# Modulation rows spread from memory, gates in ten buffers, both norms tile by tile, router with stationary weights

## The chip, the core and the metric

The kernel runs on one core of a Trainium2 chip. The metric is the time of one execution in device microseconds (us); lower is better. TensorE does the matrix products, VectorE and ScalarE the elementwise work and everything that leaves PSUM, GpSimd (POOL) small scalar work and part of the DMA issues, and SyncE (SP) issues the weight loads.

## The reference

One transformer layer over 640 tokens (128 of context, 512 latent), width 1024, in float32. The stages around the change are these:

```
mod   = silu(c) @ w_ada + b_ada            # six rows of 1024 for each of two conditions: sh1 sc1 g1 sh2 sc2 g2
z     = h @ w_in                           # queries, keys, values, and gate logits ga, gb
mix   = sigmoid(ga)*(oa @ w_proj_a) + sigmoid(gb)*(ob @ w_proj_b)
x1    = x + g1 * rms_norm(mix @ w_out, g_post_mix)
h2    = rms_norm(x1, g_pre_ffn) * (1 + sc2) + sh2
lg,le = h2 @ w_router_group, h2 @ w_router_expert      # 4 + 32 logits per token; top group, top 2 experts
y     = x1 + g2 * rms_norm(moe(h2), g_post_ffn)        # 32 SwiGLU experts of width 512
```

## The kernel before

The 640 tokens are five tiles of 128 rows (NT = 5); tile 0 is the context. Nothing is scheduled by a tool: each engine has its own hand-written program, and counting semaphores order them. TensorE executes strictly in program order, and so do the other engines. A product is done as three fp32r passes (hi x hi, lo x hi, hi x lo, L1120 to L1122). So each 1 MB piece of weights ("split" s) is first copied by ScalarE into a hi part (`split_hi`, L843) and then turned by VectorE into a lo part (`split_lo`, L1515). Four k-slices of one split against one tile are 12 matmuls with 512 moving columns.

The stages, with their place in the profiled execution:

1. Input projection and the modulation product, up to 325 us. The sigmoid gates leave PSUM through `zs` and are stored by POOL to memory (`gates_scratch`). The modulation columns are combined into `modr`, 128 x 64: four kinds of row, times two conditions, times 8 blocks.
2. Attention, 325 to 507.5 us: 40 steps (20 "diff", then 20 "swa"). The first exponential (L959) waits for the maximum (L1680) and for the landing of all stored gates; the maximum comes after a small exponential for lambda (L937).
3. TensorE spreads the modulation rows over the partitions: 12 groups of four matmuls (L1350) take one column of `modr`, broadcast to 128x128, against the identity, and ScalarE copies each bank to `brow` (L991).
4. Branch projections, splits 18 to 21, g = 0 to 3. VectorE multiplies each tile's bank by its gate (L1762, or L1765 and L1766 for the second branch). The gates come back from memory into `gst`, two buffers of 128x512, through POOL (L754): the load for tile m waits until VectorE has used tile m-2 (`mix_done`). Then ten groups of four transposes (L1377) turn the mix into columns, ScalarE makes hi (L1003), VectorE lo (L1773).
5. Out projection, splits 22 to 25, from 587.4 us. ScalarE copies each bank to `yrow` and squares it with a row sum (L1012, L1013).
6. The norms, each stage over all five tiles: VectorE adds the sums (L1779); POOL forms the inverse root by a scale and a power (L660, L661); VectorE scales by it and by the gate row g1 (L1783); POOL adds x (L764); ScalarE squares (L1020); POOL takes the second inverse root; VectorE scales and shifts (L1786, L1787); POOL stores h2 (L769).
7. Router: per tile eight transposes (L1401), two copies by ScalarE into the one buffer `h2T` (L1028), and eight float32 matmuls (L1406) that take the 128x128 block of h2 as stationary operand and move the 36 router columns. VectorE then selects experts (from L1792) and builds the gather tables.
8. Expert loop, from 735 to about 1324 us.
9. Last stage: the y pairs come back from memory, VectorE sums each pair (L1919, L1921). TensorE spreads the last gate rows g2 in four groups (L1498), and ScalarE copies them to `brow` (L1103). Behind these copies in ScalarE's program stand the squares (L1108). Then POOL's root, VectorE's scaling and addition of x (L1926, L1928), and the store.

## Time and profile before

| | us |
|---|---|
| median of 3 runs | 1379.41 |
| lowest and highest run | 1373.64, 1381.17 |
| the profiled execution's own time | 1375.16 |
| span of its trace | 1373.3 |
| TensorE busy | 1182.0 (86%) |
| VectorE busy | 866.5 (63%) |
| ScalarE busy | 695.7 (51%) |
| GpSimd busy | 324.1 (24%) |

The shares are averages over stages with different limits. The expert loop fills 43% of the span and is dense on TensorE and on the DMA engines; the stages 3 to 7, which the diff touches, take some 190 us before the first expert row table is built.

### The profile page before, as it was taken

To read this page: it belongs to the slowest core of one execution; us is meant where nothing else is said; L and a number is where in the kernel's file an instruction comes from. 1 tells how busy PE (TensorE), PEld (TensorE's weight loads), DVE (VectorE), ACT (ScalarE), POOL (GpSimd) and SP (SyncE) were. 2 spreads that over 40 slices of the span, in tenths; PEclk is the share of its full clock that TensorE was granted. 3 is DMA by queue.
4 is the path that set the end of the run, shared out by engine and by line. 5 is a ranking of instruction groups with operands and counts; after the bars stand their busy time and mean duration, and the time that the engine had idled before them with its cause. 6 is when DMAs were issued, how large, how long until landed. Compare 5 with 4: busy or idle time off the path is not lost.

```text
span 1373.3 us, 17096 instructions
## 1 busy us (share of the span) xinstructions
PE 1182.0 (86%) x6059; PEld 955.9 (70%) x6059; DVE 866.5 (63%) x941; ACT 695.7 (51%) x785; POOL 324.1 (24%) x300
## 2 busy tenths in 40 slices
PE   3889999998777989897545999999999999999941
PEld 2567787776565878785434888888888888888731
DVE  3443242124887633512554999999999999999836
ACT  3222233224544432132223777778778787787722
POOL 4022030000211001102402234444433333444200
PEclk9899999999997989998557999999999999999985
DMA  9533345551001003430134999999999999999924
GB/s 315 197 123 131 115 156 179 203 179 39 1 1 62 2 16 120 135 114 0 77 123 157 352 377 373 376 369 361 357 365 356 361 359 363 358 361 357 363 69 189
DMA packets 144845, 292.16 MB, mean 213 GB/s; under 512 B 11953, under 2 KB 13106, under 8 KB 144146
## 3 DMA queue, kind: packets, MB, share of 16 engines
q1 hardware_dynamic: 129936, 263.21, 53.9%
q0 software_dynamic: 14688, 28.12, 6.1%
q8 instruction: 37, 0.61, 0.2%
q14 instruction: 22, 0.18, 0.0%
q10 hardware_dynamic: 162, 0.05, 0.0%
HBM read 286.48 MB, written 27.92 MB: 229 GB/s over the span
## 4 chain that ended last, share of the span: by engine, by line
PE 67%; DVE 12%; ACT 7%; issue 7%; DMA 4%; POOL 1%; ACTq 0%; POOLq 0%; DVEq 0%
PE psum L1120 17%; PE psum L1122 16%; PE psum L1121 16%; DVE w_lo L1872 3%; DMA pt<-gates_scratch 2%; ACT w_hi L1038 2%; PE psum L1231 2%; PE psum L1334 2%; PE psum L1314 2%; PE psum L1138 2%; PE psum L1406 1%; ACT L1055 1%; ACT act_hi L1049 1%; PE psum L1432 1%; PE psum L1462 1%
## 5 line engine op out<-in xcount | busy, mean ns | idle before, releaser
L1120 PE MATMUL psum<-w_hi,act_hi 128*128 128x512 f32 (+1 forms) x1288 | 515.2, 400 | 21.4 <-DVE w_lo L1872 6.4
L1122 PE MATMUL psum<-w_hi,act_lo 128*128 128x512 f32 (+1 forms) x1288 | 501.6, 389 | 0.0
L1121 PE MATMUL psum<-w_lo,act_hi 128*128 128x512 f32 (+1 forms) x1288 | 500.8, 389 | 0.0
L1120 PEld LDWEIGHTS psum<-w_hi,act_hi 128*128 128x128 f32 x1288 | 244.0, 189 | 94.0 <-issue 18.1
L1122 PEld LDWEIGHTS psum<-w_hi,act_lo 128*128 128x128 f32 x1288 | 243.7, 189 | 51.2
L1121 PEld LDWEIGHTS psum<-w_lo,act_hi 128*128 128x128 f32 x1288 | 244.5, 190 | 44.7
L1872 DVE TENSOR_TENSOR w_lo<-raw_extra,w_hi 128x2048 fp32r<-128x2048 f32 x96 | 217.3, 2290 | 45.8 <-ACT w_hi L1038 45.8
L1872 DVE TENSOR_TENSOR w_lo<-raw_mix,w_hi 128x2048 fp32r<-128x2048 f32 x96 | 218.9, 2289 | 12.2 <-ACT w_hi L1038 12.1
L1038 ACT ACTIVATE w_hi<-raw_mix 128x2048 fp32r<-128x2048 f32 x96 | 183.8, 1916 | 26.7 <-PE psum L1122 26.7
L1038 ACT ACTIVATE w_hi<-raw_extra 128x2048 fp32r<-128x2048 f32 x96 | 180.7, 1913 | 6.2 <-PE psum L1122 6.2
L1515 DVE TENSOR_TENSOR w_lo<-raw_mix,w_hi 128x2048 fp32r<-128x2048 f32 (+1 forms) x26 | 57.4, 2208 | 176.1 <-ACT w_hi L843 176.1
L797 POOL DMA_INDIRECT y_scratch<-ysb,scatter_column x32 | 34.5, 1078 | 357.3 <-DVE ysb L1896 324.0
L785 POOL DMA_INDIRECT xg<-h_scratch,gather_column x32 | 71.0, 2219 | 25.5 <-POOL gather_column L782 25.5
L843 ACT ACTIVATE w_hi<-raw_mix 128x2048 fp32r<-128x2048 f32 (+1 forms) x26 | 48.0, 1846 | 49.7 <-DMA raw_mix<-in_w_in 26.6
L1314 PE MATMUL psum<-ident,rows 128*128 128x128 f32 x204 | 39.7, 303 | 25.3 <-DVE rows L529 10.2
L959 ACT ACTIVATE rows<-psum,soft 128x640 f32<-128x640 f32 (+3 forms) x80 | 50.6, 641 | 12.2 <-DVE soft L1682 7.4
L792 POOL COPY scatter_column<-scatter_rows 128x1 uint32 (+1 forms) x32 | 54.6, 1706 | 0.2
L782 POOL COPY gather_column<-gather_rows 128x1 uint32 (+1 forms) x32 | 53.1, 1658 | 5.0 <-PE psum L1432 4.9
L1049 ACT ACTIVATE act_hi<-psum 128x1024 fp32r<-128x1024 f32 x32 | 32.8, 1026 | 37.8 <-PE psum L1432 37.8
L973 ACT ACTIVATE pt<-psum 128x512 f32<-128x512 f32 (+2 forms) x36 | 18.5, 514 | 61.8 <-PE psum L1314 61.4
L1314 PEld LDWEIGHTS psum<-ident,rows 128*128 128x128 f32 x204 | 25.0, 155 | 33.4 <-issue 16.2
L1680 DVE TENSOR_REDUCE soft<-psum 128x2 f32<-128x1280 f32 (+3 forms) x40 | 44.4, 1110 | 4.6 <-PE psum L1290 2.5
(264 smaller groups left out, 1263.5 us busy)
## 6 DMA issues: line engine op xcount, KB each, us to landing
raw_mix<-in_w_e SPq DMA_DIRECT2D x96, 1024.0 KB, 8.3
raw_extra<-in_w_e SPq DMA_DIRECT2D x96, 1024.0 KB, 8.3
raw_mix<-in_w_in SPq DMA_DIRECT2D x16, 1024.0 KB, 5.9
raw_mix<-in_w_ada SPq DMA_DIRECT2D x16, 1024.0 KB, 7.3
ada_first<-in_w_ada SPq DMA_DIRECT2D x8, 1024.0 KB, 20.1
gates_scratch<-rows POOLq DMA_DIRECT2D x20, 256.0 KB, 3.3
pt<-gates_scratch POOLq DMA_DIRECT2D x20, 256.0 KB, 3.6
raw_mix<-in_w_out SPq DMA_DIRECT2D x4, 1024.0 KB, 5.1
```

What stands on the lines that cost most here:

```text
L782: po.tensor_copy(idx_g[:, par:par + 1], tab_g[:, bass.ds(n, 1)]).then_inc(gi_done, 1)
L785: po.indirect_dma_start(out=xg[:, par * D:(par + 1) * D], out_offset=None, in_=h2_d, in_offset=bass.IndirectOffsetOnAxis(idx_g[:, par:par ...
L792: po.tensor_copy(idx_s[:, par:par + 1], tab_s[:, bass.ds(n, 1)]).then_inc(si_done, 1)
L843: ac.activation(whi(s % HL)[:, :, 0:w], raw(n % RAW_MIX)[:, :, 0:w], ACT.Copy).then_inc(hi_done, 1)
L959: ac.activation(e[:, m * w:(m + 1) * w], s_view(i)[:, m, :], ACT.Exp, bias=soft[:, 16 * b + m:16 * b + m + 1], scale=SCALE, accum_out=tota ...
L1038: ac.activation(whi(hl), raw(slot), ACT.Copy).then_inc(hi_done, 1)
L1120: pe.matmul(out, a_hi(ka_), w_hi[:, kw, :], start=s, stop=False)
L1121: pe.matmul(out, a_hi(ka_), w_lo[:, kw, :], start=False, stop=False)
L1122: ins = pe.matmul(out, a_lo(ka_), w_hi[:, kw, :], start=False, stop=e)
L1314: ins = pe.transpose(bank(6)[:, x * P:(x + 1) * P], src[:, kt * P:(kt + 1) * P], ident[:, :])
L1515: ve.tensor_tensor(wlo(s % HL)[:, :, 0:w], raw(n % RAW_MIX)[:, :, 0:w], whi(s % HL)[:, :, 0:w].bitcast(F32), ALU.subtract).then_inc(lo_don ...
L1872: ve.tensor_tensor(wlo(hl), raw(slot), whi(hl).bitcast(F32), ALU.subtract).then_inc(lo_done, 1)
```

## The change

- **Modulation rows.** `modr` (columns 0 to 63) is transposed once, by TensorE between the second and the third score step of attention, copied by ScalarE to `arow` ahead of the lambda exponential, and stored by POOL to `modulation_rows_scratch` (8 x 1024). After attention POOL issues six loads that read one row of 4 KB for each of 128 partitions (512 KB each), ahead of gate load number 10. Two more such loads fetch the g2 rows after the out projection. The matmuls of L1350 and L1498 and the copies of L991 and L1103 are gone.
- **Gates.** `gst` lies in `yrow`, ten buffers. Loads 0 to 9 wait for the last diff scores; load m from 10 on waits for the use of tile m-10.
- **Mix transposes** of tile i-1 follow the product of tile i in the last group, with ScalarE's hi and VectorE's lo parts of the same tile.
- **Norms.** Each tile goes by itself: `new_x(i)` and `new_h(i)` on VectorE, the addition of x included; POOL adds the two sums and takes both roots of one column; ScalarE's square of x1 tile i-1 stands behind the copies of tile i of the last split.
- **Router.** Two `h2T` buffers and four banks for the transposes; the weights are the stationary operand (36 columns), h2 moves 128 columns; the 36x128 result is copied and transposed back. TensorE's order is written out.

The core of the diff:

```diff
-        gst = pt[:, 0:1024].rearrange("p (b n) -> p b n", b=2)
+        gst = yrow[:, :].rearrange("p (b n) -> p b n", b=GATE_SLOTS)          # GATE_SLOTS = 10
+        h2T_v = [h2T[:, :], pt[:, 0:D]]
...
 @block.gpsimd
+            po.wait_ge(b_cp, 1)
+            po.dma_start(mod_d.rearrange("r (k p) -> (r k) p", p=P), arow[0:64, 0:P]).then_inc(mod_out, 16)
...
+            for m in range(4 * NT):
+                g, i = m // NT, m % NT
+                branch, n, slot = g % 2, g // 2, m % GATE_SLOTS
+                if m == 0:
+                    po.wait_ge(s_done, NDIFF)
+                if g == 0:
+                    po.wait_ge(gate_out[i], 64)
+                if m == GATE_SLOTS:
+                    po.wait_ge(pv_done, NSTEP)
+                    po.wait_ge(mod_out, 16)
+                    for r in range(6):
+                        po.dma_start(br_v[:, r, :], mod_d[r].partition_broadcast(P)).then_inc(b_in, 16)
+                if m >= GATE_SLOTS:
+                    po.wait_ge(mix_done, m - GATE_SLOTS + 1)
+                po.dma_start(gst[:, slot, :], gates_d[...]).then_inc(g_in[slot], 16)
...
+            for i in range(NT):
+                po.wait_ge(y_cp, 5 + i + 1)
+                link(po.tensor_tensor(stat[:, i:i + 1], stat[:, 48 + i:49 + i], stat[:, 53 + i:54 + i], ALU.add))
+                rsqrt(stat[:, 8 + i:9 + i], stat[:, i:i + 1], 1, 1.0 / D).then_inc(yrs, 1)
+                po.wait_ge(x1sq, i + 1)
+                rsqrt(stat[:, 40 + i:41 + i], stat[:, 32 + i:33 + i], 1, 1.0 / D).then_inc(x1rs, 1)
+                if i:
+                    store_h2(i - 1)
+            store_h2(NT - 1)
+            po.wait_ge(tile_mm, 5 * NS)
+            for r in range(2):
+                po.dma_start(g2_v[:, r, :], mod_d[6 + r].partition_broadcast(P)).then_inc(g2_in, 16)
...
 @block.scalar
+            ac.wait_ge(b_tr, 1)
+            ac.activation(arow[0:64, 0:P], bank(7)[0:64, 0:P], ACT.Copy).then_inc(b_cp, 1)
             ac.wait_ge(lam_sum, 1)
             ac.activation(lamv[:, 2:4], lamv[:, 0:2], ACT.Exp).then_inc(lam_exp, 1)
...
+            for i in range(NT):
+                merged_rows(1, i)
+                if i:
+                    x1_squares(i - 1)
+            h2_columns(0)
+            h2_columns(1)
+            x1_squares(NT - 1)
+            h2_columns(2)
+            logit_rows(0)
+            h2_columns(3)
+            for i in range(1, NT - 1):
+                logit_rows(i)
+            h2_columns(NT - 1)
+            logit_rows(NT - 1)
...
 @block.tensor
             scores(1)
+            pe.wait_ge(mod_done, 1)
+            pe.transpose(bank(7)[0:64, 0:P], modr[:, :], ident[:, :]).then_inc(b_tr, 1)
             scores(2)
...
-            for m in range(12):                      # and four matmuls each: modr column, identity
...
+                    if g == 3 and i:
+                        transpose_mix(i - 1)
+            transpose_mix(NT - 1)
...
+            def router(i):
...
+                    ins = pe.matmul(bank(2 + i % 2)[0:NR, 0:P], wr_v[:, k, :], h2T_v[i % 2][:, k * P:(k + 1) * P], ...)
+            def logits(i):
+                pe.wait_ge(rt_cp, i + 1)
+                pe.transpose(bank(7)[:, i * NR:(i + 1) * NR], rlT[...], ident[0:NR, 0:NR]).then_inc(rl_done, 1)
+            transpose_h2(0); transpose_h2(1); router(0); transpose_h2(2); router(1); logits(0)
+            transpose_h2(3); router(2); logits(1); router(3); logits(2); logits(3)
+            transpose_h2(4); router(4); logits(4)
...
 @block.vector
+            def new_x(i):
+                ve.wait_ge(yrs, i + 1)
+                link(ve.scalar_tensor_tensor(yr[:, i, :], yr[:, i, :], stat[:, 8 + i:9 + i], br_v[:, min(i, 1), :], ...))
+                ve.wait_ge(x2_in[i], 16)
+                ve.tensor_tensor(xrow[:, i, :], xrow[:, i, :], yr[:, i, :], ALU.add).then_inc(x1_done, 1)
+            def new_h(i):
+                ve.wait_ge(x1rs, i + 1)
+                link(ve.scalar_tensor_tensor(yr[:, i, :], xrow[:, i, :], stat[:, 40 + i:41 + i], br_v[:, 2 + min(i, 1), :], ...))
+                ve.tensor_tensor(yr[:, i, :], yr[:, i, :], br_v[:, 4 + min(i, 1), :], ALU.add).then_inc(h2_done, 1)
+            ve.wait_ge(b_in, 16 * 6)
+            for i in range(NT):
+                new_x(i)
+                if i:
+                    new_h(i - 1)
+            new_h(NT - 1)
+            ve.wait_ge(h2t_done, 2 * NT)
+            ve.wait_ge(rt_mm, NT - 2)
+            ve.tensor_copy(h2T_v[(NT - 1) % 2][:, 512:1024], bank(h2_bank(NT - 1, 1))).then_inc(h2t_v, 1)
```

## Rows read from the trace of the kernel before

**Rows 1.** The page: the span, and the granted TensorE clock in 40 slices.
```profile
span 1373.3 us, 17096 instructions
...
PEclk9899999999997989998557999999999999999985
```

**Rows 2.** Chain that ended last, whole span: start us, length us, what.
```profile
326.16 2.62 DMA gates_scratch<-rows
...
507.58 13.19 PE psum L1350 x96
...
691.89 1.77 PE psum L1401 x8
694.33 3.64 PE psum L1406 x16
...
1343.91 5.80 PE psum L1498 x32
```

**Rows 3.** Waits from 505 to 740: total us, times, longest.
```profile
DVE rows L1762 <- DMA pt<-gates_scratch: 17.7, 6, 5.3
...
DVE osq L1765 <- DMA pt<-gates_scratch: 10.3, 6, 3.2
```

**Rows 4.** Busy time and granted clock by stretch, seven columns of the windows view.
```profile
508.00:510.00 2.00, 2.00 (x11) 2.00 (x11) 0.69 (x1) 0.43 (x2) 0.00 (x0) 0.50 0.32 119
...
512.00:514.00 2.00, 2.00 (x20) 2.00 (x19) 0.00 (x0) 1.18 (x2) 0.00 (x0) 1.00 0.00 0
...
690.00:698.00 8.00, 7.28 (x33) 6.73 (x33) 0.00 (x1) 1.19 (x2) 0.00 (x0) 0.50 0.30 82
```

**Rows 5.** ScalarE in order of time, from 505 to 740.
```profile
631.24 0.60 ACT L1012 ACTIVATE yrow<-psum 128x512 f32<-128x512 f32 x1 [13.19 <-PE psum L1122]
...
642.12 0.60 ACT L1012 ACTIVATE yrow<-psum 128x512 f32<-128x512 f32 x1 [1.40 <-PE psum L1122]
```

**Rows 6.** VectorE in order of time, from 505 to 740.
```profile
675.95 1.22 DVE L1787 TENSOR_TENSOR yrow<-yrow,brow 128x1024 f32<-128x1024 f32 x1
698.00 0.35 DVE L1792 TENSOR_TENSOR router_logits<-psum,br 128x180 f32<-128x180 f32 x1 [20.82 <-PE psum L1406]
```

**Rows 7.** One line's instructions: duration ns minimum, median, maximum.
```profile
L1783 DVE SCALAR_TENSOR_TENSOR yrow<-yrow,stat,brow x5: 1280/3356/3364, 645.2 to 654.2; 128x1024 f32<-128x1024 f32 x5
...
L764 POOL TENSOR_TENSOR rows<-rows,yrow x5: 2340/3313/3319, 646.6 to 659.7; 128x1024 f32<-128x1024 f32 x5
```

**Rows 8.** Groups of GpSimd instructions: busy us, mean ns of one.
```profile
L661 POOL TENSOR_TENSOR stat<-stat,half 128x5 f32<-128x5 f32 x4 | 4.8, 1194 | 0.3
...
L769 POOL DMA_DIRECT2D h_scratch<-yrow x5 | 2.8, 555 | 10.5 <-DVE yrow L1787 10.5
...
L660 POOL TENSOR_SCALAR stat<-stat 128x5 f32<-128x5 f32 x4 | 0.8, 196 | 93.6 <-DVE stat L1779 55.3 <-ACT pt L1108 29.1 <-ACT squares_scratch_a L863 8.0
```

**Rows 9.** DMA issues: KB each, median us to landing.
```profile
pt<-gates_scratch POOLq DMA_DIRECT2D x20, 256.0 KB, 3.6
...
rows<-in_x_sample POOLq DMA_DIRECT2D x4, 512.0 KB, 4.4
...
lam<-in_lam_q POOLq DMA_DIRECT2D x2, 32.0 KB, 5.7
```

**Rows 10.** ScalarE, then VectorE, from 322 to 350.
```profile
325.89 1.28 ACT L937 ACT_TABLE_LOAD   x1
...
329.26 0.37 ACT L959 ACTIVATE rows<-psum,soft 128x128 f32<-128x128 f32 x1 [1.88 <-DVE soft L1682]
...
327.42 0.16 DVE L1672 TENSOR_TENSOR lamv<-lamv 128x1 f32<-128x1 f32 x1 [11.16 <-ACT lamv L937]
```

**Rows 11.** ScalarE, then VectorE, from 1308 to the end.
```profile
1355.18 1.06 ACT L1108 ACTIVATE pt<-raw_extra 128x1024 f32<-128x1024 f32 x1
1356.14 0.19 ACT L1108 ACTIVATION_READ_ACCUMULATOR pt<-raw_extra 128x1 f32 x1
...
1352.22 1.28 DVE L1921 SCALAR_TENSOR_TENSOR raw_extra<-raw_extra,pair_weights 128x1024 f32<-128x1024 f32 x1
```

More of the change, by code:

```diff
@@ L986, in _ @@
                 attention_hi(ac, q)
[L989 to L999 removed]
+            for x in range(20, 24):
+                split_hi(x)
             for m in range(2 * NT):
@@ L1096, in _ @@
                     a_round(r)
-            for m in range(4):
-                ac.wait_ge(g2_mm, m + 1)
-                if m == 0:
-                    ac.wait_ge(all_scattered, 1)
-                ac.activation(br_v[:, m // 2, (m % 2) * 512:(m % 2) * 512 + 512], bank(m), ACT.Copy).then_inc(g2_cp, 1)
             for i in range(NT):
@@ L1340, in _, with transpose_mix @@
                 out_transpose(pe, q_)
-            pe.wait_ge(mod_done, 2)
             wait_emptied(pe, len(uses) - 1)
-            for m in range(12):
-                if m >= 2:
-                    pe.wait_ge(b_cp, m - 1)
-                for x in range(4):
-                    col = (m // 2) * 8 + (m % 2) * 4 + x
-                    ins = pe.matmul(bank(5 + m % 2)[:, x * P:(x + 1) * P], modr[:, col:col + 1].broadcast_to([P, P]), ident[:, :], start=True, stop=True)
-                ins.then_inc(b_tr, 1)
+            def transpose_mix(i):
+                pe.wait_ge(mix_done, 15 + i + 1)
+                for m in range(2 * i, 2 * i + 2):
+                    if m < 3:
+                        pe.wait_ge(o_cp, NOUT)
+                    else:
+                        pe.wait_ge(mh_done, m - 2)
+                        pe.wait_ge(ml_done, m - 2)
+                    for x in range(4):
+                        k = 4 * (m % 2) + x
+                        ins = pe.transpose(bank(5 + m % 3)[:, x * P:(x + 1) * P], xrow[:, i, k * P:(k + 1) * P], ident[:, :])
+                    ins.then_inc(mt_done, 1)
             for g in range(4):
@@ new lines, in router @@
+            def router(i):
+                pe.wait_ge(h2t_cp, min(2 * i + 2, 2 * NT - 1))
+                if i == NT - 1:
+                    pe.wait_ge(h2t_v, 1)
+                if i >= 2:
+                    pe.wait_ge(rt_cp, i - 1)
+                for k in range(KD):
+                    ins = pe.matmul(bank(2 + i % 2)[0:NR, 0:P], wr_v[:, k, :], h2T_v[i % 2][:, k * P:(k + 1) * P], start=(k == 0), stop=(k == KD - 1))
+                ins.then_inc(rt_mm, 1)
+            def logits(i):
+                pe.wait_ge(rt_cp, i + 1)
+                pe.transpose(bank(7)[:, i * NR:(i + 1) * NR], rlT[:, i % 2 * P:(i % 2 + 1) * P], ident[0:NR, 0:NR]).then_inc(rl_done, 1)
@@ L1409, in _ @@
+            transpose_h2(0)
+            transpose_h2(1)
+            router(0)
+            transpose_h2(2)
+            router(1)
+            logits(0)
+            transpose_h2(3)
+            router(2)
+            logits(1)
+            router(3)
+            logits(2)
+            logits(3)
+            transpose_h2(4)
+            router(4)
+            logits(4)
             pe.wait_ge(m_ready, 1)
@@ L1492, in _ @@
                     a_round(r)
-            pe.wait_ge(all_scattered, 1)
-            for m in range(4):
-                for x in range(4):
-                    col = 48 + (m // 2) * 8 + (m % 2) * 4 + x
-                    ins = pe.matmul(bank(m)[:, x * P:(x + 1) * P], modr[:, col:col + 1].broadcast_to([P, P]), ident[:, :], start=True, stop=True)
-                ins.then_inc(g2_mm, 1)
         @block.vector
@@ L1749, in _, with mix_low @@
                 attention_lo(ve, q)
+            def mix_low(i):
+                for m in range(2 * i, 2 * i + 2):
+                    j = m % 2
+                    ve.wait_ge(mh_done, m + 1)
+                    d = (slice(None), slice(4 * j, 4 * j + 4), slice(i * P, (i + 1) * P))
+                    ve.tensor_tensor(al[d], bank(5 + m % 3).rearrange("p (k n) -> p k n", k=4), ah[d].bitcast(F32), ALU.subtract).then_inc(ml_done, 1)
             split_lo(20)
```

182 lines of the change are left out of this document (70 added, 112 removed).

## Prediction

> **What bounds the kernel now.** I read the page first: a span of 1373.3 us, and a TensorE clock that falls in three places, early in attention, around 640 to 740 us and at the end [rows 1]. The diff leaves the expert loop alone, so the question is what it takes out of the stretch from 505 to 740 us and out of the tail. Therefore the chain that ended last comes next [rows 2]. The 48 matmuls that spread the modulation rows stand on it with 13.19 us, each tile of the router with 1.77 us of transposes and 3.64 us of products, and the last spreading with 5.80 us. The waits say what stops the branch projections: VectorE waits 17.7 + 10.3 = 28.0 us in all for gates to land [rows 3], because with two buffers each load of 3.6 us [rows 9] is issued only when the gate two tiles back has been used. The norms are a chain by nature; here all five tiles pass each stage before the next begins. From the last product (642.12, when ScalarE can take its bank [rows 5]) to the router logits on VectorE (698.00 [rows 6]) TensorE does nothing but the router, and 55.9 us pass. That is the largest piece to win.
>
> **Attention's start (loss of 0.6).** TensorE's one transpose and ScalarE's copy now stand ahead of ScalarE's table load of 1.28 us and the lambda exponential. They need the second score step, so VectorE gets lambda about 1.4 us later than its 327.42 [rows 10]. But the first exponential, at 329.26 [rows 10], was released by the last gate store, which left at 326.16 and took 2.62 us [rows 2], to 328.8. VectorE's maximum was ready some 0.8 us before the exponential. So about 0.6 of the 1.4 us comes through; between 0 and 3 us, the upper end if the longer pause makes the clock dip last longer. All later steps shift by it. The store of 64 rows on POOL and the first ten gate loads, about 0.55 us of POOL each, run under attention, where POOL has nothing else but one head norm per tile.
>
> **From attention to the out projection (gain 17.4).** The 13.19 us [rows 2] go. The products then start at 507.6 in the same low clock: 0.50 from 508 to 510, 1.00 from 512 [rows 4]. What ran slowly there was the spreading; now it is products, and about 3.9 us at half rate cost them 2.0 us. A tile of a split takes (642.12 - 631.24) / 4 = 2.72 us at full clock [rows 5], so 20 tiles of branch projection take 54.4 us. The 20 tiles of the out projection took as long before 642.1, so that stage began at 587.7, and the stretch before it, from 507.6, took 80.1 us. In its place stand 54.4 + 2.0, then 40 transposes, at half of the 0.22 us that one takes at the low clock (1.77 / 8 [rows 2]), 4.4, and about 1.9 us of stalls: the first mix tile must wait for split 23's lo part, and the last tile's transposes wait for its own mix, two VectorE operations of some 0.7 us (half of the 1.22 for 1024 columns [rows 6]) and one ScalarE copy of 0.60 [rows 5]. Sum 62.7, gain 17.4. Interleaved transposes could stall up to 1 us a tile more, or nothing; I keep 14 to 19.
>
> This needs gate 10 by about 540 and the modulation rows by about 617. POOL issues six broadcast loads at 505, then the gates as their buffers come free. A plain load of 512 KB lands after 4.4 us, while a small one that repeats a row (32 KB in 256-byte pieces) takes 5.7 us [rows 9]. No row shows a broadcast with 4 KB pieces. Like plain loads, six are over 10 to 27 us after their issue, by 532. By bytes at the rate of the 32 KB load, one would take 91 us. I take the plain load: the piece is 4 KB in both, while the 5.7 us of the small load are nearly the same as the 4.4 us of one sixteen times its size and so tell of a fixed cost. Hidden then, with 8 us or more to spare.
>
> **Out projection and norms.** The projection is untouched and ends at 642.1 - 17.4 + 0.6 = 625.3; the last split's tile 0 is ready at 614.4. ScalarE needs about 1.3 us for copy and square (0.60 each, and a readout). POOL's first root is now an addition and a scale of 0.2 each and a power of 1.19 [rows 8], 1.8 us with its links. For one column I assume what five columns cost, since 0.2 us for five values is all fixed cost. So VectorE's `new_x(0)` starts at 617.5 and takes 1.28 + 1.22 = 2.5 [rows 6, 7]. The addition of x, 2.3 to 3.3 us on POOL [rows 7], has become 1.22 on VectorE.
>
> Then each tile is a circle, because POOL's program puts the second root of tile i before the first root of tile i+1: new_x 2.5, square 1.3 (1.06 and 0.19 [rows 11]), root 1.55, store of h2 0.65 (0.555 [rows 8] and its link), first root of the next 1.8: 7.8 us. Meanwhile VectorE runs `new_h` of the tile before, 2.5 us. Do they disturb each other? Rows 7 show it: VectorE's scaling takes 1.28 us alone and 3.36 beside POOL's addition, and POOL's addition 2.34 alone and 3.31 beside VectorE. Each is longer by what was left of the other. So POOL's root, which would begin 1.3 us after new_x, begins when new_h is over, 2.5 us after it: 9.0 us a circle.
>
> The Trainium skill (SBUF — State Buffer, "SBUF: two separate sides") says the same: a VectorE operation with two SBUF inputs and a GpSimd operation that reads SBUF shut each other out for a whole instruction. This rule speaks against the new order; without it the circle is 7.8.
>
> With 9.0: new_x(1) at 624.7 (no new_h or store yet), the next at 633.7, 642.7 and 651.7; new_h(3) to 656.7, the last root to 658.3, new_h(4) to 660.8. Before, the last h2 tile was ready at 675.95 + 1.22 = 677.2 [rows 6]. So of the 16.8 us won earlier 16.4 are left here: the norms are no shorter in themselves, but the router can start inside them.
>
> **Router.** ScalarE's copies of h2 tiles 0 and 1 stand behind the square of x1 tile 3 (to 646.5), so the first product starts at 647.8. A product moves 128 columns in eight matmuls. From the spreading, 48 matmuls of that shape in 13.19 us, 3.9 of them at half rate [rows 2, 4], one is 0.23 us at full and 0.46 at low clock: 1.8 or 3.6 us a tile. At the low clock that is nothing won over the 3.64 [rows 2]. All at low clock: products 0 and 1 to 656.8, tile 3's transposes (1.8 us) behind new_h(3), products 2 and 3 to 666.8, tile 4's transposes to 669.3, a copy, product 4 to 673.6, copy and transpose back: 674.4. At full clock from the second product on, the two late tiles bound it: 666.6. Which? The old router, with 36 moving columns, was busy 7.28 of 8 us and stayed at 0.50 [rows 4]; the spreading, 128 columns without a break, rose to 1.00 after about 4 us [rows 4]. Here tiles 0 to 2 are 9 us without a break, but then comes a pause of 2 to 3 us. I take the middle, 670.5: gain at this point 698.0 - 670.5 = 27.5.
>
> The skill's page TensorE: Matmul & The Clock Gate (Part 1) lets the clock follow how busy TensorE is. By that the old router too should have run at 1.00, and rows 4 contradict it; by the page the new one ends at 666.6, and the sum would be 4 us better.
>
> **Expert tables, loop and tail.** The tables and the gathers follow VectorE's logits unchanged. SP's loads into the overlapped buffers now wait for all router logits instead of the transposed copies, still some 26 us before the tables are ready. The loop is the same. In the tail VectorE's last pair sum ends at 1352.22 + 1.28 = 1353.5 [rows 11]; the last square then ends at 1354.8 instead of 1356.37: gain 1.6. The 5.80 us of spreading were mostly under the loads of y, so more isn't to be had.
>
> **Sum.** 27.5 + 1.6 = 29.1. On the profiled execution's 1375.2 (span 1373.3 and 1.9 around it) this gives 1346.1; the median of the runs, 1379.4, is 4.2 higher, and with it 1350.3. I predict 1350.
>
> **Rivals.**
> - *No shutting out.* POOL's small operations slip in beside new_h: circle 7.8, the router starts 2.3 us earlier and at full clock ends at 663. Gain 32 to 36, time 1343 to 1347. For it: these operations are short. Against: rows 7. Chance 0.22.
> - *A leaner win.* The attention dip costs 3, stalls in the last branch group 3, the low clock holds through the router: gain 14 to 22, time 1357 to 1365. Chance 0.15.
> - *Broadcast loads are slow* (the side slower than before). Gate 10 and its followers stand behind six loads on one queue. If each takes t, gate 10 lands at 505 + 6t + 4; it is needed at 540, so loss begins at t = 5 us if they don't overlap, and eats the whole 29 us at t = 10 us. Slower by over 0.5% from t = 11. At the 91 us of the upper bound the time would be near 1860. For it: nothing but that no row has such a load. Chance 0.06; a further 0.05 that it, or the circle of five engines' waits, leaves the gain between -7 and 7.
> - The forecast, 1346 to 1356: chance 0.52.
>
> About 0.5%, 7 us, is what a measurement can tell from no change. Faster 0.89, same 0.06, slower 0.05. The range of 1340 to 1363 takes in the first two rivals and the bounds of the clock and leaves out the slow loads.
>
> **What the new profile would show.** Products start within 1 us of attention's last copy; no VectorE wait for gates; the out projection starts near 571; new_x starts 8 to 9 us apart, with POOL's scale right behind new_h; the first router product near 648; VectorE's logits near 670 (667 if the clock row shows 1.00, 674 if 0.50); the expert loop as long as before. I am wrong if gates after number 9 are waited for, if new_x starts are 11 us apart, or if the loop's length changes.

## The result and the profile after

The changed kernel takes 1335.5 us in the median of four runs (1331.97 to 1336.06), the kernel before 1379.3 beside it: ratio 0.968 with a 95% interval of 0.965 to 0.972. The profiled execution took 1335.54 us, 39.6 less than that of before, and its span is 39.7 shorter. I had predicted 1350 with a range of 1340 to 1363, so the time is lower than the range.

To see where the 39.7 us lie, both spans are cut at the same instructions: ScalarE's last copy of a gate bank (325.27 before), VectorE's last copy of attention (506.74), ScalarE's copy of the last split's tile 0 (631.24 in [rows 5]), VectorE's logits (698.00 in [rows 6]), and the end. The cuts that no row above shows, kernel before (ScalarE, then VectorE) and changed kernel:

```profile
325.27 0.60 ACT L929 ACTIVATE rows<-psum 128x512 f32<-128x512 f32 x1 [2.12 <-PE psum L1122]
506.74 0.69 DVE L531 COPY rows<-psum 128x512 f32<-128x512 f32 x1 [1.21 <-PE psum L516]
```
```profile
322.78 0.60 ACT L950 ACTIVATE rows<-psum 128x512 f32<-128x512 f32 x1 [2.12 <-PE psum L1152]
...
508.18 0.69 DVE L538 COPY rows<-psum 128x512 f32<-128x512 f32 x1 [1.21 <-PE psum L523]
...
615.03 0.60 ACT L1024 ACTIVATE yrow<-psum 128x512 f32<-128x512 f32 x1 [13.19 <-PE psum L1152]
```

| stretch | before | after | difference | predicted |
|---|---|---|---|---|
| start to last gate copy | 325.27 | 322.78 | -2.5 | 0 |
| to attention's last copy | 181.47 | 185.40 | +3.9 | +0.6 |
| to the last split's tile 0 | 124.50 | 106.85 | -17.65 | -17.4 |
| to the router logits | 66.76 | 45.82 | -20.9 | -10.7 |
| to the end | 675.30 | 672.75 | -2.55 | -1.6 |
| sum | 1373.3 | 1333.6 | -39.7 | -29.1 |

The page of the changed kernel: the span and the granted TensorE clock in 40 slices. Against [rows 1] the dip around 640 to 700 is one slice shorter, and the middle of attention is a little lower.

```profile
span 1333.6 us, 16867 instructions
...
PEclk9899999999887898999858999999999999999985
```

VectorE in order of time, changed kernel, from 612 to 665. It answers [rows 6] and the first line of [rows 7]:

```profile
617.67 1.28 DVE L1833 SCALAR_TENSOR_TENSOR yrow<-yrow,stat,brow 128x1024 f32<-128x1024 f32 x1 [13.50 <-POOL stat L669]
...
630.84 1.28 DVE L1833 SCALAR_TENSOR_TENSOR yrow<-yrow,stat,brow 128x1024 f32<-128x1024 f32 x1 [2.45 <-POOL stat L669]
...
634.62 1.23 DVE L1840 TENSOR_TENSOR yrow<-yrow,brow 128x1024 f32<-128x1024 f32 x1
...
638.30 1.28 DVE L1833 SCALAR_TENSOR_TENSOR yrow<-yrow,stat,brow 128x1024 f32<-128x1024 f32 x1 [2.46 <-POOL stat L669]
...
660.85 0.34 DVE L1855 TENSOR_TENSOR router_logits<-psum,br 128x180 f32<-128x180 f32 x1 [2.66 <-PE psum L1446]
```

`new_x` (L1833) comes every 638.30 - 630.84 = 7.46 us, not every 9.0. Each time VectorE has waited some 2.45 us for GpSimd's root. (The first two, with no `new_h` or store between them, are 5.73 us apart, where I had 7.2.) What GpSimd does in one such circle (L781 adds the sums, L668 is the scale, L669 the power, L777 the store), changed kernel, GpSimd in order of time:

```profile
634.66 1.23 POOL L668 TENSOR_SCALAR stat<-stat 128x1 f32<-128x1 f32 x1 [3.85 <-ACT pt L1031]
635.97 0.54 POOL L669 TENSOR_TENSOR stat<-stat,half 128x1 f32<-128x1 f32 x1
636.48 0.63 POOL L777 DMA_DIRECT2D h_scratch<-yrow  x1
637.14 0.20 POOL L781 TENSOR_TENSOR stat<-stat 128x1 f32<-128x1 f32 x1
637.43 0.19 POOL L668 TENSOR_SCALAR stat<-stat 128x1 f32<-128x1 f32 x1
637.70 0.56 POOL L669 TENSOR_TENSOR stat<-stat,half 128x1 f32<-128x1 f32 x1
```

Two things are to be read here. The power takes 0.55 us where [rows 8] had 1.19 for five columns. And the same scale takes 0.19 us at 637.43, when VectorE is idle, but 1.23 at 634.66: it ends at 635.89, just after VectorE's L1840 (634.62 to 635.85) does. GpSimd was shut out while VectorE read two tensors, as forecast from [rows 7]. The Trainium skill (SBUF — State Buffer, "SBUF: two separate sides") says this of just such a pair; the trace agrees, with 1.23 against 0.19.

TensorE in order of time, changed kernel, from 634 to 662, and its clock by stretch (busy time of PE, PEld, DVE, ACT, POOL, then the granted clock, DMA share, GB/s), against the last lines of [rows 2] and [rows 4]:

```profile
643.05 3.29 PE L1441 MATMUL psum<-h2T,wr 128*36 128x128 f32 x16 [3.68 <-ACT h2T L1038]
...
647.30 1.94 PE L1441 MATMUL psum<-pt,wr 128*36 128x128 f32 x16
650.65 0.25 PE L1446 MATMUL psum<-ident,orow 36*128 36x36 f32 x1 [1.41 <-ACT orow L1052]
...
658.30 1.91 PE L1441 MATMUL psum<-h2T,wr 128*36 128x128 f32 x16 [0.83 <-ACT h2T L1038]
```
```profile
644.00:646.00 2.00, 2.00 (x12) 1.69 (x11) 0.25 (x1) 0.00 (x0) 1.51 (x4) 0.53 0.45 182
646.00:648.00 2.00, 2.00 (x19) 1.64 (x17) 1.97 (x2) 0.00 (x0) 0.00 (x0) 1.00 0.20 80
648.00:650.00 2.00, 1.23 (x12) 0.97 (x9) 1.97 (x3) 1.68 (x4) 0.44 (x1) 1.00 0.00 0
```

The first product stands behind a pause of 3.68 us, in which the clock fell (1.00 until 642.4, 0.50 from there), and runs at half rate. From 646 on the clock is 1.00, the products take 1.9 us, and the later pauses (the longest 1.41 us, before 650.65) do not bring it down.

DMA issues of the changed kernel: KB each and median us to landing. The six broadcast loads of `brow`, issued within 3.2 us, land 4.4 to 9.9 us after issue, in the median 6.4. That is somewhat longer than the 4.4 us of the plain loads in [rows 9], and nowhere near the 91 us of the upper bound. From 505 to 662 VectorE does not wait for a gate any more ([rows 3] had 28.0 us of it).

```profile
yrow<-gates_scratch POOLq DMA_DIRECT2D x20, 256.0 KB, 6.0
brow<-modulation_rows_scratch POOLq DMA_DIRECT2D x6, 512.0 KB, 6.4
last_gate_rows<-modulation_rows_scratch POOLq DMA_DIRECT2D x2, 512.0 KB, 5.4
```

### The profile page after: what moved, and what is told of

Its sections match the earlier page's. It is cut to its first block, busy times and chain, and to the rows that moved or that the text cites. A ratio compares the mean times of both kernels' runs of the same rounds, so it can differ in the third digit from the quotient of the medians.

```text
span 1333.6 us, 16867 instructions
## 1 busy us (share of the span) xinstructions
PE 1161.0 (87%) x5937; PEld 933.2 (70%) x5937; DVE 867.5 (65%) x946; ACT 685.9 (51%) x774; POOL 325.1 (24%) x325
## 4 chain that ended last, share of the span: by engine, by line
PE 71%; DVE 11%; ACT 7%; issue 6%; DMA 3%; POOL 1%; ACTq 0%; POOLq 0%; SPq 0%; DVEq 0%
PE psum L1150 19%; PE psum L1152 18%; PE psum L1151 18%; PE psum L1261 3%; DVE w_lo L1935 3%; PE psum L1346 2%; PE psum L1368 2%; ACT w_hi L1073 2%; PE psum L1168 2%; PE psum L1487 1%; ACT L1090 1%; DMA raw_extra<-y_scratch 1%; ACT act_hi L1084 1%; PE psum L1517 1%; DVE rows L1746 1%
## 5 line engine op out<-in xcount | busy, mean ns | idle before, releaser
L1150 PEld LDWEIGHTS psum<-w_hi,act_hi 128*128 128x128 f32 x1288 | 244.4, 190 | 94.7 <-issue 18.2
L1935 DVE TENSOR_TENSOR w_lo<-raw_extra,w_hi 128x2048 fp32r<-128x2048 f32 x96 | 217.2, 2289 | 45.8 <-ACT w_hi L1073 45.8
L982 ACT ACTIVATE rows<-psum,soft 128x640 f32<-128x640 f32 (+3 forms) x80 | 50.6, 640 | 10.3 <-DVE soft L1730 5.3
L1102 ACT ACTIVATE act_hi<-psum 128x512 fp32r<-128x512 f32 x32 | 19.2, 599 | 54.8 <-PE psum L1517 54.8
```

Of the source, the lines that this page charges most:

```text
L982: ac.activation(e[:, m * w:(m + 1) * w], s_view(i)[:, m, :], ACT.Exp, bias=soft[:, 16 * b + m:16 * b + m + 1], scale=SCALE, accum_out=tota ...
L1150: pe.matmul(out, a_hi(ka_), w_hi[:, kw, :], start=s, stop=False)
L1935: ve.tensor_tensor(wlo(hl), raw(slot), whi(hl).bitcast(F32), ALU.subtract).then_inc(lo_done, 1)
```

## The experiments

Each group of runs that was compared had its own runs of the kernel before beside it, and the ratios are to those. The last five columns are cut like the table above, from each run's own profile.

| run | median us | ratio to before, 95% | gate copy | attention | to last split | to logits | to end |
|---|---|---|---|---|---|---|---|
| changed, first profile | 1335.5 | 0.968 (0.965-0.972) | 322.8 | 185.4 | 106.9 | 45.8 | 672.8 |
| changed again | 1336.7 | 0.972 (0.970-0.974) | 324.5 | 185.3 | 106.8 | 45.8 | 672.5 |
| before again | 1377.9 | 1.001 (0.999-1.004) | 324.7 | 181.3 | 127.6 | 66.8 | 675.2 |
| roots on five columns | 1341.9 | 0.974 (0.973-0.976) | 325.3 | 185.5 | 106.9 | 51.5 | 673.4 |
| h2 stationary | 1340.4 | 0.974 (0.972-0.976) | 322.6 | 183.3 | 106.8 | 51.4 | 673.9 |
| two gate buffers | 1345.1 | 0.978 (0.976-0.980) | 324.3 | 185.5 | 114.5 | 45.8 | 672.5 |
| six rows by TensorE | 1348.6 | 0.980 (0.979-0.982) | 324.7 | 185.2 | 117.9 | 45.8 | 672.7 |
| modulation part undone | 1346.6 | 0.979 (0.976-0.981) | 324.8 | 181.3 | 118.1 | 45.8 | 675.1 |
| mix transposes last | 1338.1 | 0.971 (0.968-0.974) | 325.0 | 185.4 | 107.9 | 45.8 | 672.2 |
| copy behind | 1334.2 | 0.971 (0.968-0.973) | 322.8 | 179.0 | 106.6 | 45.9 | 672.4 |
| first roots ahead | 1333.3 | 0.970 (0.968-0.972) | 324.9 | 185.3 | 106.9 | 40.2 | 673.1 |
| both of these | 1330.2 | 0.967 (0.965-0.969) | 323.0 | 183.4 | 107.9 | 40.7 | 673.3 |
| both, wide matmuls | 1327.9 | 0.965 (0.963-0.967) | 324.9 | 179.2 | 106.5 | 40.3 | 672.8 |

Among the versions of the changed kernel whose edit leaves it alone, the stretch to the last split is 106.5 to 106.9 us (once 107.9, in "both of these", where the low clock at its start costs 1 us more) and the stretch to the logits 45.8 to 45.9. Their last stretch wanders from 672.2 to 673.9, the first one from 322.6 to 325.3. The kernel before is less steady: its stretch to the last split took 124.5 us in one profile and 127.6 in the other. There TensorE waited 5.2 and 8.1 us at the mix transposes, against 0.9 in the changed kernel. So the gain of this stretch is 17.65 us in the first pair of profiles and 20.7 in the second. An edit is judged by its own stretch first and by the whole time second. Each version but these two kernels has one profile.

**The power's cost.** Was the circle short because one column is cheap?

```diff
+            def rsqrt_wide(k, in_):
+                w = wroot[:, 5 * k:5 * k + 5]
+                link(po.tensor_scalar(w, in_.broadcast_to([P, 5]), 1.0 / D, EPS, ALU.mult, ALU.add))
+                return po.tensor_tensor(w, w, half[:, 0:5], ALU.pow)
-                rsqrt(stat[:, 8 + i:9 + i], stat[:, i:i + 1], 1, 1.0 / D).then_inc(yrs, 1)
+                rsqrt_wide(2 * i, stat[:, i:i + 1]).then_inc(yrs, 1)        # and the second root alike
```

> Edit to the changed kernel: GpSimd forms both inverse roots of each tile on five equal columns instead of one; nothing else differs. Theory (the cost of the power goes by its columns, and the circle of the norms contains both roots): a power takes about 1.2 us instead of 0.55, the start of new_x is 8.4 to 8.8 us apart instead of 7.45, the router logits reach VectorE about 4 to 6 us later, and the time is 3 to 6 us above the changed kernel, near 1340. Rival (the short circle has another cause, the power costs the same on one and on five columns here): power 0.55, circle 7.45, time within 2 us of the changed kernel. Second rival (the power is longer, but VectorE's new_h covers it): power 1.2, circle 7.5 to 7.8, time within 2 us.

GpSimd with both roots on five columns, in order of time:

```profile
631.72 1.24 POOL L783 TENSOR_SCALAR wide_roots<-stat 128x5 f32<-128x5 f32 x1 [3.85 <-ACT pt L1038]
633.04 1.16 POOL L784 TENSOR_TENSOR wide_roots<-wide_roots,half 128x5 f32<-128x5 f32 x1
```

The power is 1.16 to 1.19 us, the scale is the same as for one column (1.24 shut out, 0.20 alone), `new_x` starts 8.73 us apart, and the logits come 5.7 us later after the last split. The theory held, and both rivals fell: the power is on the path, and five columns cost more than one.

**What lets the clock rise in the router.**

```diff
-                    ins = pe.matmul(bank(2 + i % 2)[0:NR, 0:P], wr_v[:, k, :], h2T_v[i % 2][:, k * P:(k + 1) * P], ...)
+                    ins = pe.matmul(bank(7)[:, i * NR:(i + 1) * NR], h2T_v[i % 2][:, k * P:(k + 1) * P], wr_v[:, k, :], ...)
```

> Edit to the changed kernel: the router's products again take the h2 block as stationary operand and move the 36 router columns, in the new order of TensorE and of the norms; the copy of the 36 x 128 result and its transposition back are gone. Theory W (the wide moving operand is what lets the granted clock rise to 1.00 in the router): clock 0.50 from the first product to the logits, 3.6 us a product, logits on VectorE about 8 to 10 us later, time 5 to 10 us above the changed kernel, 1341 to 1346. Rival D (dense work is enough, whatever its width; before, the pauses between tiles kept the clock low): clock 1.00 from the third tile on, 1.8 us a product, time within 3 us of the changed kernel, since copy and transposition back (some 1.5 us) are saved too.

TensorE's clock by stretch, with h2 stationary, columns as before:

```profile
642.00:644.00 2.00, 2.00 (x11) 2.00 (x12) 0.58 (x1) 0.00 (x0) 1.19 (x4) 0.50 0.61 250
...
650.00:652.00 2.00, 2.00 (x12) 2.00 (x11) 1.64 (x2) 1.20 (x2) 0.02 (x1) 0.50 0.65 262
...
656.00:658.00 2.00, 2.00 (x11) 2.00 (x11) 0.00 (x0) 0.00 (x0) 0.00 (x0) 0.50 0.84 342
```

From 642 to 658 TensorE shows no pause at all and stays at 0.50; a product takes 3.5 to 3.6 us. The changed kernel, with 128 moving columns, went to 1.00 in the same place, pauses and all. So the pauses were not what kept the old router slow: rival D fell. The edit swaps both operands, though. It does not tell the width of the moving one (36 or 128) from that of the stationary one (128 or 36). The logits come 5.55 us later, not 8 to 10; part of that difference is the saved copy and transposition back. The median, 1340.4, lies just below the range of theory W, and in this profile attention took 183.3 us, 2 us less than in the other versions that start it alike. The Trainium skill (TensorE: Matmul & The Clock Gate, Part 1) lets the clock follow how busy TensorE is; if busy is what the profile counts, this run, busy 2.00 of 2.00 us at 0.50, does not bear that out, and neither did [rows 4].

**Ten gate buffers.**

```diff
-GATE_SLOTS = 10
+GATE_SLOTS = 2
```

> Edit to the changed kernel: two gate buffers instead of ten (the load for tile m waits for the use of tile m-2, as before); the six broadcast loads keep their place ahead of load 10. Theory A (a tile of the product takes 2.7 us on TensorE and a gate comes back 3.6 us after its issue, so most of the wait lies under the products, and the branch stage is set by TensorE): the stage from the first product to the out projection grows by 3 to 8 us over 62.5, time 1338 to 1344; the six broadcasts behind a late load can add up to 5. Rival B (the waits of VectorE that the ten buffers took away, 28 us before, were on the path): the stage grows by 15 to 28 us, time 1350 to 1363. Rival C: nothing changes, the ten buffers were worth nothing, time within 2 us.

Waits from 505 to 600 with two buffers: total us, times, longest.

```profile
DVE rows L1818 <- DMA yrow<-gates_scratch: 10.8, 5, 5.0
...
PE psum L1389 <- DVE rows L1822: 6.7, 2, 6.0
...
DVE osq L1821 <- DMA yrow<-gates_scratch: 6.6, 2, 3.4
```

VectorE waits for gates again, 10.8 + 6.6 = 17.4 us, but TensorE only 6.7 (0.9 with ten buffers), and the stretch grows by 114.54 - 106.83 = 7.7 us. Most of VectorE's wait lies under the products; what counts is where TensorE waits for VectorE, at the mix transposes of the end. Theory A held, at the upper end of its range for the stage and 1 us above it in time (1345.1). But the run tests the two buffers together with the place of the broadcasts: the six loads now go out between gate loads 9 and 10, and the longest wait is for gate 10:

```profile
551.50 0.69 DVE L1818 TENSOR_TENSOR rows<-psum,yrow 128x512 f32<-128x512 f32 x1 [4.96 <-DMA yrow<-gates_scratch]
```

How much of the 7.7 us is this collision, which the kernel before did not have, is not separated.

**The spreading by TensorE.** Twelve groups of four matmuls between attention and the products, with ScalarE's copies, in place of the six loads:

```diff
+            for m in range(12):
+                for x in range(4):
+                    ins = pe.matmul(bank(5 + m % 2)[:, x * P:(x + 1) * P], modr[:, col:col + 1].broadcast_to([P, P]), ident[:, :], ...)
+                ins.then_inc(s_tr, 1)
```

> Edit to the changed kernel: the six modulation rows are again spread by TensorE, 12 groups of four matmuls between attention and the branch products, with ScalarE's copies of each bank, and the six loads from memory are left out; the transposed store and the two g2 loads stay. Theory A (these 13.2 us stood on the path, and only the low clock that they carried moves to the products): the stage from attention's end to the out projection grows from 62.5 to 73.7, that is by 11 us, time 1345 to 1348. Rival B (ScalarE's and VectorE's preparation of split 18 sets when the products can start, and hides the spreading): grows by less than 4 us, time 1336 to 1340. Rival C: it grows by the whole 13.2 us or more, time 1349 or above.

TensorE at the end of attention in that run:

```profile
510.65 13.06 PE L1385 MATMUL psum<-ident,modr 128*128 128x128 f32 x96 [0.78 <-DVE rows L539]
523.46 0.47 PE L1152 MATMUL psum<-w_hi,act_hi 128*128 128x512 f32 x1
```

The stretch is 117.85 - 106.83 = 11.0 us longer, as theory A said: 13 us of matmuls, of which 2 were only the low clock, which the products carry in the changed kernel. The median, 1348.6, is 0.6 us above theory A's range.

**The interleaved mix transposes.**

```diff
-                    if g == 3 and i:
-                        transpose_mix(i - 1)
-            transpose_mix(NT - 1)
+            for i in range(NT):
+                transpose_mix(i)                      # VectorE's mix_low likewise behind its gate products
```

> Edit to the changed kernel: the 40 transposes of the mix stand behind all products of the last branch group again, and VectorE's low parts behind all its gate products. Theory (the interleaving only fills TensorE's waits, and the transposes cost their own time either way): the stage from attention's end to the last split grows by 0 to 2 us over 106.8. Rival (the copies and low parts of the last tiles come onto the path when they all stand at the end): it grows by 3 to 8 us, time 3 to 8 us higher.

107.91 against 106.83: the interleaving is worth 1.1 us. The run with both late edits, which leaves this part alone, has 107.87, so the difference has to be placed: there the extra 1 us stands before VectorE's third gate product, here it comes after the seventeenth (95.8 us from the third gate product to the cut in both the changed kernel and that run, 96.9 here). The theory held. Eleven, 7.7 and 1.1 make 19.8, between the 17.65 us of the first pair of profiles and the 20.7 of the second. The tests are too coarse to say that the three parts add up.

**Attention's extra 3.9 us.** I had allowed 0.6. First, was it the kernel or the execution? Both kernels ran again:

> The changed kernel once more, unedited, beside the runs below: 1331 to 1337 us. It is there to compare with, and to see whether attention's length (185.4 us from ScalarE's last gate copy to the last copy of attention, against 181.5 before) and its clock of 0.83 come again: if the kernel's new start of attention sets them, 185 and 0.83; if they vary from execution to execution, anything from 181 to 186.

> The kernel before once more, unedited, for a second profile of its attention. In its first profile attention took 181.5 us from ScalarE's last gate copy to the last copy of attention, while the changed kernel took 185.3 to 185.5 in two of its own profiles and in three of edits that leave attention alone, and 183.3 in one. If the change itself makes attention longer: 181 to 182 again. If the length varies from execution to execution in both kernels: 183 to 186 is as likely.

The clock in the same 40 us of attention: kernel before, second profile, then the changed kernel, second profile.

```profile
382.00:422.00 40.00, 29.13 (x228) 23.26 (x226) 32.03 (x90) 20.87 (x54) 7.96 (x15) 0.96 0.00 1
```
```profile
382.00:422.00 40.00, 32.47 (x213) 26.57 (x212) 29.78 (x75) 17.89 (x47) 6.64 (x12) 0.79 0.00 1
```

181.3 and 185.3 came again. The kernel sets it in the main, and the clock (0.96 against 0.79, 228 matmuls against 213) is where it shows. It is not a fixed number: of the eight profiles with attention's start as changed, seven have 185.2 to 185.5 and one, h2 stationary, has 183.3. Then the modulation part was undone as a whole, the last g2 rows too:

```diff
-            pe.transpose(bank(7)[0:64, 0:P], modr[:, :], ident[:, :]).then_inc(b_tr, 1)
-            ac.activation(arow[0:64, 0:P], bank(7)[0:64, 0:P], ACT.Copy).then_inc(b_cp, 1)
-            po.dma_start(mod_d.rearrange("r (k p) -> (r k) p", p=P), arow[0:64, 0:P]).then_inc(mod_out, 16)
...                                                   # rows by TensorE as above; g2 in the last stage:
+            pe.wait_ge(all_scattered, 1)
+            for m in range(4):
+                for x in range(4):
+                    ins = pe.matmul(bank(m)[:, x * P:(x + 1) * P], modr[:, col:col + 1].broadcast_to([P, P]), ident[:, :], ...)
+                ins.then_inc(b_tr, 1)
```

> Edit to the changed kernel: the whole modulation part is undone. No transposition, copy and store at the start of attention; the six rows are spread by TensorE before the branch products, and the two g2 rows by TensorE and ScalarE in the last stage. Ten gate buffers, norms and router stay as changed. Theory (the early transposition and copy make attention longer, by 0.67 us at its first exponential and by some 3 us more through a lower TensorE clock): attention 181 to 182 instead of 185.3, the stage behind it 117.9 instead of 106.8, the tail 1.5 to 3 us longer, so that the whole part is worth 8 to 10 us, time 1344 to 1347 against 1336.7. Rival (attention's length has nothing to do with it): attention 184.5 to 185.5, the part worth 12 to 14 us, time 1348 to 1351.

Attention was 181.3 us at a clock of 0.96 again, the branch stretch 118.1, the end 675.1 against 672.5. The theory held: the part gives 11.2 + 2.5 and takes 4.0, that is 9.8 us, and the medians differ by 1346.6 - 1336.7 = 9.9. Of the 2.5 us 2.0 lie behind VectorE's last pair sum, where g2 is used; the rest is within what the last stretch wanders. The third way at it was to move ScalarE's copy alone:

```diff
-            ac.wait_ge(b_tr, 1)
-            ac.activation(arow[0:64, 0:P], bank(7)[0:64, 0:P], ACT.Copy).then_inc(b_cp, 1)
             ac.wait_ge(lam_sum, 1)
             ac.activation(lamv[:, 2:4], lamv[:, 0:2], ACT.Exp).then_inc(lam_exp, 1)
+            ac.wait_ge(b_tr, 1)
+            ac.activation(arow[0:64, 0:P], bank(7)[0:64, 0:P], ACT.Copy).then_inc(b_cp, 1)
```

> Edit to the changed kernel: ScalarE copies the transposed modulation rows behind the lambda exponential instead of ahead of it. Theory (the copy and its wait for TensorE put off the first exponential of attention, and through it the whole): the first exponential comes 4.0 instead of 4.66 us after ScalarE's last gate copy, and all follows, time 0.6 to 1.4 us lower. Second theory (the longer pause also sets the lower clock of attention): attention 2 to 4 us shorter, time 3 to 5 us lower. Rival (the gates' landing or TensorE sets the start): no change, within 1 us.

The first exponential came 3.70 us after the gate copy instead of 4.66, and in this profile attention took 179.0 us. The median is 2.5 us below the changed kernel's, between the two theories. But the six runs range from 1328.7 to 1338.5 and the intervals of this run and of the changed kernel overlap; with the same start of attention, the two versions below had 183.4 and 179.2. So the first exponential's 1.0 us is shown, the rest is not: attention comes in lengths of about 179, 181, 183 and 185 us. Its mean granted clock is 0.90 in the shortest, 0.88 at 181 and 0.83 to 0.85 in the two longest. With this copy moved, three profiles have 179.0, 179.2 and 183.4; with the copy ahead no profile is under 183.

**What the circle of the norms still costs.** GpSimd took the second root of tile i before the first root of tile i+1:

```diff
-            for i in range(NT):
+            first_root(0)
+            for i in range(NT):
+                if i + 1 < NT:
+                    first_root(i + 1)                 # then the second root of tile i and the store, as before
```

> Edit to the changed kernel: in GpSimd's program the first inverse root of tile i+1 stands ahead of the second root of tile i. Theory A (the circle of 7.45 us exists because the two roots are bound to each other by GpSimd's order; without it VectorE's new_x and new_h, 5 us a tile, or the last split's tiles on TensorE set the pace): new_x starts 5 to 6.5 us apart, h2 of the last tile 5 to 9 us earlier, and since the router's five tiles then run closer together on TensorE, the logits 3 to 7 us earlier; time 3 to 7 us lower. Rival B (the router on TensorE is the bound at once): h2 earlier, but the logits within 2 us, time within 2 us. Rival C (ScalarE's square or the shutting out takes over): circle 7 or more, no change.

GpSimd and then VectorE, in order of time, with the first roots ahead:

```profile
630.61 1.53 POOL L669 TENSOR_TENSOR stat<-stat,half 128x1 f32<-128x1 f32 x1
...
634.85 0.56 POOL L669 TENSOR_TENSOR stat<-stat,half 128x1 f32<-128x1 f32 x1
```
```profile
630.51 1.22 DVE L1840 TENSOR_TENSOR rows<-rows,yrow 128x1024 f32<-128x1024 f32 x1
...
632.17 1.28 DVE L1844 SCALAR_TENSOR_TENSOR yrow<-rows,stat,brow 128x1024 f32<-128x1024 f32 x1 [0.44 <-POOL stat L669]
```

`new_x` now starts 6.2 us apart and the logits come 5.6 us earlier after the last split; the time fell by 3.3 us, the low end of theory A. (The medians fell by less than the stretch; this profile's last stretch is 0.6 us longer, in a part that the edit does not touch.) VectorE works 5.0 us of each 6.2. The rest is the shutting out, which now strikes GpSimd more often: the power that takes 0.56 alone takes 1.53 beside L1840, and VectorE waits for it. GpSimd shows busy for 5.9 of each 6.25 us, for operations that take some 2.3 us alone. The two edits together:

> Both edits together (GpSimd's first roots ahead, ScalarE's copy of the modulation rows behind the lambda exponential). The two act in different stages, so their gains should add: 4 to 8 us below the changed kernel if each holds, 0 to 2 if neither.

1330.2 us, 6.5 below the changed kernel run beside it, which is the sum of the two (2.5 + 3.3) within what the runs can tell. On top of it TensorE's pause before the router was filled with work that nobody reads:

```diff
+            for _ in range(24):
+                pe.matmul(bank(7)[:, 0:P], ident[:, :], ident[:, :], start=True, stop=True)
             transpose_h2(0)
             transpose_h2(1)
```

> Edit to the version with GpSimd's first roots ahead and ScalarE's copy behind: TensorE runs 24 matmuls that nobody reads (identity times identity, 128 moving columns) between the last product of the out projection and the transposes of h2, so that its pause of 6 us is filled. Theory (the transposes of tiles 0 and 1 and the first product run at the low clock only because of that pause): the clock stays 1.00 from the out projection through the router, the transposes of two tiles take 2.0 instead of 3.6 us and the first product 1.9 instead of 2.8, the logits come 1 to 2.5 us earlier, time 1 to 2.5 us lower than 1330.2. Rival (h2 of the last tile sets the logits, and TensorE has time to spare): clock 1.00, logits within 0.5 us. Second rival (the clock falls all the same in the router's pauses): no change or a loss.

TensorE of that run in order of time:

```profile
627.73 1.94 PE L1437 MATMUL psum<-ident,yrow 128*128 128x128 f32 x16 [1.01 <-ACT osq L1031]
633.66 3.20 PE L1447 MATMUL psum<-h2T,wr 128*36 128x128 f32 x16 [3.99 <-ACT h2T L1044]
636.78 1.45 PE L1437 MATMUL psum<-ident,yrow 128*128 128x128 f32 x8
```

The clock of that run by stretch, columns as before:

```profile
632.00:634.00 2.00, 0.34 (x3) 0.35 (x4) 1.97 (x2) 2.00 (x6) 1.88 (x3) 1.00 0.50 207
634.00:636.00 2.00, 2.00 (x12) 1.70 (x11) 1.27 (x2) 0.58 (x2) 1.83 (x3) 0.54 0.14 55
```

The transposes of two tiles took 1.94 instead of 3.6 us. But the first product did not start sooner: it waits for ScalarE's copy of h2 and begins 23.1 us after the last split's tile 0, in this run as in the two before it. And the clock, 1.00 through the pause of 3.99 us, fell half a microsecond into this product. The logits came 40.25 us after the last split's tile 0, where first roots ahead alone had 40.24 and both edits 40.67. So the theory failed, and both rivals had a part: TensorE had time to spare before the product, and the clock fell all the same. The matmuls gave nothing that can be told from the 0.4 us between the two versions without them. The run's median, 1327.9, is the lowest here, but its profile has the short attention of 179.2, and its interval (0.963 to 0.967) overlaps that of the version without them (0.965 to 0.969). It would not be right to credit the matmuls with it.

## Why the prediction was wrong

The direction, the places of the gain and the order of the stages were right. The time was 14.8 us too high: 10.6 in the sum, and 4.2 in the step from the profiled execution to the median.

- **Attention's start: wrong by 3.3 us, against the gain.** The 0.6 us at the first exponential came out as 0.67 (4.66 against 3.99 behind the gate copy). The clock's part, which stood only at the upper end of the bound (3 us), is real and larger: 185.3 against 181.3 in repeated profiles, with one of 183.3 among the eight.
- **Attention to out projection: right, with some luck in the last digit.** The stretch gave 17.65 us against 17.4, but 20.7 by the second pair of profiles, since the kernel before varies here by 3.1. The spreading bears its single test: 11.0 (13.2 less 2.0). The gates are less clean, 7.7 with the broadcasts in the way. The broadcast loads landed after 6.4 us in the median, near the plain loads' 4.4 of [rows 9], and the rival of slow broadcasts fell.
- **The circle of the norms: the step that failed.** "For one column I assume what five columns cost, since 0.2 us for five values is all fixed cost": the scale, on whose row this rested, costs the same at both widths, and the power does not; it took 0.55, not 1.19. Two powers in each circle are 1.3 of the 1.55 us between 9.0 and 7.45. With five columns put back, the circle is 8.73 and the logits 5.7 us later: this one term is over half of the 10.3 us by which this stretch was off. That the operations shut each other out, the doubtful part of the step, was right; the rival without it had a circle of 7.8 us, nearer to 7.45, for a wrong reason, and a time of 1343 to 1347, still too high.
- **The router's clock: the middle was the wrong value.** The logits with five-column roots came 51.5 us after the last split's tile 0. The bound at full clock from the second product on was 666.6 - 614.4 = 52.2, the low-clock bound 60.0, and I took the middle, 56.1. In that run the clock was 1.00 from the second product on. So 3.9 us are the clock, and 0.7 the rest. The row for the rise, the spreading with the same 128 moving columns, was there; the pauses that made me doubt it were 1.4 us at most, not 2 to 3, and did no harm.
- **Tail: right.** From the end of VectorE's last pair sum to the end of the span it was 19.8 us before (1373.3 - 1353.5) and 18.2 changed: the 1.6 us of the forecast. With the g2 loads undone it is 20.2. The other 0.9 of the 2.55 us lie between the logits and that pair sum, a part that wanders between 653.9 and 655.6 us in the profiles.
- **The input stage** was 2.5 us shorter in the profile of after. No edit touches it, and it ends between 322.6 and 325.3 in all the profiles here: most likely a chance of two executions, not a gain.
- **From the profiled execution to the median: +4.2 was a mistake of size.** The three runs had a median of 1379.4; later groups of the same kernel have 1374.4 (17 runs), 1375.8 (11), 1376.1 (9) and 1377.9 (8), the first three near the profiled 1375.2. The changed kernel's profiled execution was at its own median. Beside the 11 it gained 39.2 us, what the traces say. Three runs were too few for a term of 4 us.

Put together, from 1350.3: -4.2 for the median, -5.7 for the power, -3.9 for the clock, -0.7 for the rest of this stretch, -0.2 for the branch stretch, -1.0 for the last stretch (not its tail), -2.5 for the input stage, +3.3 for attention: 1335.4.

The sum closes because each stretch is taken from the one pair of profiles. The 2.5 us of the input stage, which nearly cancel the miss in attention, are chance as far as is known. One thing stays open: how a pause or an operation of a microsecond at the start of attention chooses among its four lengths. That the part of the diff at this place makes it longer is shown; which instruction decides is not.

## What to carry to other kernels

A price taken from a wider or narrower shape needs to be split into a fixed part and a part by size for that very operation; another operation's fixed cost says nothing about it, and in a circle of waits the error counts once for each turn. When the two ends of a bound are two states of a clock, ask for each which row resembles the new code most, and forecast one of them with the other as rival; the middle stands for neither. And judge an edit on its own stretch between two fixed instructions, before the whole time, which wanders by several microseconds. Here such a stretch mostly repeats to 0.4 us, but not always: the kernel before moved by 3.1 us in one. So take a second profile of both kernels before a forecast of a stretch is called right.

## What the runs showed that I had not expected

- GpSimd's power costs 0.55 us on one column and 1.17 on five, while its scale costs 0.19 and 0.20. An estimate from these two widths is 0.15 us for each further column of 128 values.
- TensorE ran 16 us without a pause at the low clock (0.50, the 1.2 GHz level) when the moving operand of its products was 36 columns wide, and rose to 1.00 in the same place with 128 moving columns, where pauses of up to 1.4 us did not bring it down. In the changed kernel the clock fell within the pause of 3.68 us before the first product; with the wide matmuls it fell 0.5 us behind the end of the pause of 3.99.
- Attention takes one of about four lengths, 179, 181.4, 183.4 and 185.4 us. With one copy and one transposition at its start, 0.67 us on the path, it took 4.0 us longer in seven of eight profiles and 2.0 in one.
